# Decay rows of a state-space scan: from matmuls into PSUM to a DRAM round trip and GpSimd

## The reference, cut to what matters

```python
adt = (dt * a).reshape(b, nc, L, g, j)            # decay per token and head
acs = jnp.cumsum(adt, axis=2)                      # running sum in the chunk
tri = jnp.tril(jnp.ones((L, L), dtype=bool))
seg = acs[:, :, :, None] - acs[:, :, None, :]
decay = jnp.exp(jnp.where(tri[None, None, :, :, None, None], seg, -jnp.inf))
cb = jnp.einsum('bclgn,bcsgn->bclsg', cc, bc)
y_diag = jnp.einsum('bclsgj,bcsgjp->bclgjp', cb[..., None] * decay, xdt)
...
y_off = jnp.einsum('bclgn,bcgjpn,bclgj->bclgjp', cc, prev_states, jnp.exp(acs))
```

## Time and profile before

| | |
|---|---|
| median of 3 runs | 1867.87 us (1867.15 to 1870.73) |
| the profiled execution | 1866.71 us, of it span 1864.9 us |
| TensorE's granted clock over the span | 0.995 of full |
| PE busy | 1811.9 us (97%), 11428 matmuls |
| DVE busy | 1301.9 us (70%) |
| ACT busy | 924.2 us (50%) |
| POOL busy | 552.9 us (30%) |
| the stage of the change | 245 to 307 us from the span's start |

### The profile page before, as it was taken

The page is one execution under the profiler, slowest core; times in us unless marked ns, Lnnn a source line. Parts: engine busy times, 40 slices in busy tenths (PEclk is TensorE's granted clock), DMA queues, the critical chain, the costliest instruction groups (busy, mean ns, idle before and its releaser), DMA issues.

```text
span 1864.9 us, 33412 instructions
## 1 busy us (share of the span) xinstructions
PE 1811.9 (97%) x11428; PEld 1576.3 (85%) x11428; DVE 1301.9 (70%) x2376; ACT 924.2 (50%) x1296; POOL 552.9 (30%) x247
## 2 busy tenths in 40 slices
PE   9999999999999989999999999999999999989997
PEld 6899977896878989999999988888886677659996
DVE  4667497775424599357777588888886687867777
ACT  5565544533556534467777543333334474134444
POOL 5867643500668598810000000000000000003333
PEclk9999999999999999999999999999999999999999
DMA  6544433577344467755555787777777880155553
GB/s 213 196 149 143 169 107 102 192 248 240 124 167 152 140 187 220 210 175 179 171 176 175 204 260 233 241 235 235 238 238 256 267 282 19 57 189 183 183 188 113
DMA packets 122841, 347.67 MB, mean 186 GB/s; under 512 B 13904, under 2 KB 46800, under 8 KB 122512
## 3 DMA queue, kind: packets, MB, share of 16 engines
q1 hardware_dynamic: 121248, 339.52, 55.9%
q0 software_dynamic: 1520, 7.21, 1.1%
HBM read 328.84 MB, written 17.83 MB: 186 GB/s over the span
## 4 chain that ended last, share of the span: by engine, by line
PE 82%; DVE 7%; POOL 4%; ACT 3%; issue 3%; DMA 1%; POOLq 0%; ACTq 0%; DVEq 0%
PE banks L915 81%; POOL weight_rest L825 4%; DMA weight_ring<-in_stream 1%; ACT arena L1552 1%; ACT weight_high L1552 1%; PE banks L926 1%; DVE ssd_rest L2150 1%; DVE arena L2320 1%; DVE weight_rest L2124 0%; DVE arena L2691 0%; DVE arena L2806 0%; DVE small L2700 0%; DVE attention_rest L2379 0%; DVE arena L2269 0%; DVE arena L2103 0%
## 5 line engine op out<-in xcount | busy, mean ns | idle before, releaser
L1552 ACT ACTIVATE weight_high<-weight_ring 128x1024 fp32r<-128x1024 f32 x448 | 473.2, 1057 | 451.8 <-PE banks L915 374.4
L825 POOL TENSOR_TENSOR weight_rest<-weight_ring,weight_high 128x1024 fp32r<-128x1024 f32 x181 | 469.5, 2604 | 199.8 <-ACT weight_high L1552 116.4
L2124 DVE TENSOR_TENSOR weight_rest<-weight_ring,weight_high 128x1024 fp32r<-128x1024 f32 x267 | 326.8, 1224 | 165.9 <-ACT weight_high L1552 161.8
L915 PE MATMUL banks<-a_high,weight_high 128*128 128x256 f32 x1216 | 303.8, 288 | 0.1
L915 PE MATMUL banks<-a_rest,weight_high 128*128 128x256 f32 x1216 | 297.8, 283 | 0.0
L915 PEld LDWEIGHTS banks<-a_rest,weight_high 128*128 128x128 f32 x1216 | 233.0, 192 | 0.3 <-issue 0.2
L915 PEld LDWEIGHTS banks<-a_high,weight_high 128*128 128x128 f32 x1216 | 232.6, 191 | 0.6 <-ACT weight_high L1552 0.3
L915 PE MATMUL banks<-weight_high,gated_high 128*128 128x512 f32 x512 | 201.4, 393 | 0.0
L915 PE MATMUL banks<-weight_high,gated_rest 128*128 128x512 f32 x512 | 200.2, 391 | 0.0
L1552 ACT ACTIVATE arena<-banks 128x512 f32<-128x512 f32 (+4 forms) x241 | 161.0, 689 | 65.4 <-PE banks L915 63.4
L915 PE MATMUL banks<-a_high,weight_rest 128*128 128x256 f32 x1216 | 171.9, 284 | 12.4 <-POOL weight_rest L825 12.4
(11 more groups left out here) (319 smaller groups left out, 3223.6 us busy)
## 6 DMA issues: line engine op xcount, KB each, us to landing
weight_ring<-in_stream SPq DMA_DIRECT2D x512, 512.0 KB, 3.5
arena<-in_stream SPq DMA_DIRECT2D x66, 512.0 KB, 3.3
unit_spill<-small SPq DMA_DIRECT2D x128, 128.0 KB, 3.6
scratch<-unit_spill SPq DMA_DIRECT2D x128, 128.0 KB, 3.2
residual<-in_x SPq DMA_DIRECT2D x2, 512.0 KB, 4.3
arena<-in_mem POOLq DMA_DIRECT2D x2, 512.0 KB, 5.1
arena<-in_ctx POOLq DMA_DIRECT2D x2, 512.0 KB, 5.0
arena<-in_keys POOLq DMA_DIRECT2D x1, 1024.0 KB, 5.2
```

The lines of the kernel that those rows point to most:

```text
L825: nc.gpsimd.tensor_tensor(w_lo[:, e % 2, :], raw(e)[0], w_hi[:, e % 2, :], ALU.subtract).then_inc(S["rest_ready"], 1)
L915: return nc.tensor.matmul(out, lhsT, rhs, start=start, stop=stop, skip_group_check=True)
L1552: return nc.scalar.activation(out, in_, f, **kw)
L2124: tt(w_lo[:, e % 2, :], raw(e)[0], w_hi[:, e % 2, :], ALU.subtract).then_inc(S[ready], 1)
```

## The change

The "row" matmuls, VectorE's `decay_rows` and GpSimd's `adt_rows` go. In their place:

- TensorE does two small matmuls ("acr") behind "acs", ADT of a chunk times `upto`, which give the running sums with a head per partition (32 x 128 for each chunk). ScalarE evacuates them to ACR, between two weight splits and the second half of the attention's exponentials.
- GpSimd stores ACR to DRAM in two DMAs (`decay_rows`, 8 x 1024 floats), behind the rest split of tile 17 of `in_xbc`.
- For each group GpSimd issues a DMA that reads the group's 1024 floats for all 128 partitions into DROW (`scratch`, two buffers, 512 KB each time). Those of groups 0 and 1 are issued behind tile 20.
- GpSimd does the subtraction and the bound by 0 (`decays(k)`, 8 instructions of 128 x 128, SBUF to SBUF), then issues the load of group k + 2. The rest split of `mem_k` 0 comes behind `decays(1)`.
- ScalarE's exponential waits for `decays_made` and no longer for the row banks. The turns of the banks are kept: where a row took one, the turn is left out.

```diff
@@ plan_banks
     B.job("acs")
+    B.job("acr")
...
-            turn("row", *groups[k], 0)
-            turn("row", *groups[k], 1)
+            next(turns)
+            next(turns)
@@ gpsimd
-            def adt_rows(k):
+            def load_decay_rows(k):
+                if k > 1:
+                    pool.wait_ge(S["decays_made"], k - 1)
+                pool.dma_start(DROW[:, k % 2].rearrange("p h l -> p (h l)"),
+                               decay_rows[k].partition_broadcast(P)).then_inc(rows_in[k % 2], 16)
+            def decays(k):
                 c, g = k // SG, k % SG
+                pool.wait_ge(rows_in[k % 2], 16 * (k // 2 + 1))
                 if k > 1:
-                    arrived(pool, ("row", (k - 2) // SG, (k - 2) % SG, 1))
-                nc.gpsimd.tensor_copy(ADTB[:, k % 2], bc(ADT[:, c, 8 * g:8 * g + 8], 2, P)).then_inc(S["adtb_ready"], 1)
+                    arrived(pool, ("yd", (k - 2) // SG, (k - 2) % SG))
+                for j in range(8):
+                    h = 8 * g + j
+                    ins = nc.gpsimd.tensor_scalar(EM[:, k % 2, j, :], DROW[:, k % 2, j, :], ACS[:, c, h:h + 1], 0.0,
+                                                  ALU.subtract, ALU.min)
+                ins.then_inc(S["decays_made"], 1)
...
-            pool.wait_ge(S["adt_ready"], 1)
-            adt_rows(0)
-            for n in range(18, 24):
+            freed(pool, ("acr",))
+            for c in range(TT):
+                pool.dma_start(decay_rows[c * SG:(c + 1) * SG].rearrange("g (h l) -> (g h) l", h=8),
+                               ACR[:, c, :]).then_inc(rows_out, 16)
+            for n in range(18, 21):
                 split_rest(E0["in_xbc"] + n)
-            adt_rows(1)
-            split_rest(E0["mem_k"])
-            for k in range(2, TT * SG):
-                adt_rows(k)
+            pool.wait_ge(rows_out, 16 * TT)
+            load_decay_rows(0)
+            load_decay_rows(1)
+            for n in range(21, 24):
+                split_rest(E0["in_xbc"] + n)
+            pool.wait_ge(S["acs_ready"], 1)
+            for k in range(TT * SG):
+                decays(k)
+                if k + 2 < TT * SG:
+                    load_decay_rows(k + 2)
+                if k == 1:
+                    split_rest(E0["mem_k"])
@@ tensor
+            b = claim(("acr",))
+            for c in range(TT):
+                ins = mm(b[0:32, c * P:(c + 1) * P], ADT[:, c, :], C("upto"))
+            filled(ins, ("acr",))
...
-                if k < len(groups):
-                    c, g = groups[k]
-                    pe.wait_ge(S["adtb_ready"], k + 1)
-                    for half in range(2):
-                        b = claim(("row", c, g, half))
-                        for j in range(4):
-                            ins = mm(b[:, hsl(j)], ADTB[:, k % 2, 4 * half + j, :], C("upto"))
-                        filled(ins, ("row", c, g, half))
@@ scalar
+            evacuate(("acr",), ACR.rearrange("p c l -> p (c l)"), src=lambda b: b[0:32, 0:T])
             attention_exp(1)
...
-                for half in range(2):
-                    freed(act, ("row", k // SG, k % SG, half))
+                act.wait_ge(S["decays_made"], k + 1)
                 func(EM[:, k % 2], EM[:, k % 2], ACT.Exp).then_inc(S["seg_exp"], 1)
@@ vector
             for k in range(n_groups + 1):
-                if k < n_groups:
-                    decay_rows(k)
```

## The result

The changed kernel is slower: 1880.55 us as a median (1878.44 to 1882.88, four runs) against 1868.14 (1867.15 to 1870.73, four runs), and that is clear of noise: a ratio of 1.0061 with a 95% interval of 1.0045 to 1.0077. On another chip it came to 1877.63 against 1868.33, 1.0047 (1.003 to 1.0064). The forecast was 1858 with a range of 1852 to 1868.5. The profiled execution has 1879.72 us, 13.0 more than that of the kernel before. I look for these 13 us first.

What follows compares the result with a forecast made beforehand. It took TensorE to bound the loop's second half, VectorE and ScalarE the first. Terms: -13.8 + 0.8 + 2.0 + 0.9 = -10.1 us, from 1866.71 to 1856.6; median 1.16 higher, rounded 1858, range 1852 to 1868.5.

Steps and rivals of the forecast that it cites:

- The subtraction: One GpSimd `tensor_scalar` of 128 columns in the loop: 0.40 us, so 3.2 us a group.
- The waits for VectorE: GpSimd waits for VectorE's instructions with two SBUF inputs, 0.6 us a group, making `decays` 3.8 us.
- two loops through buffers, EM's and DROW's: Buffer reuse over two groups: EM's 8.1 us against TensorE's 9.12, DROW's 9.8 us.
- the slow-GpSimd rival: GpSimd's subtractions hold up the loop: old beat equalled at 1.0 us each, 1886 at 1.5 us; chance 0.11.
- The middle rival: Loads come late, or a subtraction takes 0.6 to 0.9 us, shrinking the gain: 1862 to 1868; chance 0.18.
- the DROW loop: Load issue, landing and subtractions take 9.8 us in two groups, 0.33 a group over TensorE: 2.0 us over six groups.
- its store and its first loads: DRAM store and loads of groups 0 and 1, ahead of the loop: covered by rest splits, cost nothing.
- TensorE's side: Without the row matmuls a group costs TensorE 4.56 us; the loop ends at 293.3, not 307.1, 13.8 us earlier.
- "Acr" and what goes with it: Added matmuls on TensorE, 0.5 us, and their evacuation on ScalarE, 0.4: 0.9 us slower.
- The port: Up to 260 us VectorE waits for GpSimd's rest split of `mem_k` 0 and one decay: 0.8 us slower.

Runs made afterwards that it cites:

- experiment 8: Changed kernel with GpSimd subtracting four heads of a group and ScalarE four, loads from GpSimd: 1863.95 us, ratio 0.9978; run again 1865.32 us, 0.9976.
- the best version: Changed kernel with four subtractions a group on GpSimd, four on ScalarE, loads of groups 2 to 7 from ScalarE's queue: 1859.71 us, ratio 0.9952.
- experiment 2: Changed kernel with VectorE subtracting from the loaded rows, GpSimd only issuing loads, rest split of `mem_k` 0 moved ahead: 1865.70 us, ratio 0.9994.
- experiment 7: Changed kernel with ScalarE making difference and bound from the loaded rows in SBUF, GpSimd only issuing loads: 1863.95 us, ratio 0.9982.
- experiment 4: Changed kernel with another form of GpSimd instruction in most groups, to price each form: one time, 1857.68 us.
- experiment 1: Changed kernel with two GpSimd instructions of 1024 columns a group in place of eight of 128: 1869.36 us, ratio 1.0013.
- experiment 6: Kernel before, row matmuls kept, with ScalarE making difference and bound from PSUM in place of VectorE: 1868.63 us, ratio 1.0001.
- experiment 11: Changed kernel with the loads of groups 2 to 7 issued from ScalarE's queue, all subtractions on GpSimd: 1872.32 us, ratio 1.0035.
- experiment 10: Changed kernel with 6, 6 and 8 filler matmuls in TensorE's last three waits only: 1873.93 us, ratio 1.0034.
- experiment 9: Filler matmuls before each group's products in the changed kernel: 1882.90 us, ratio 1.0072; in groups 0 to 3 of experiment 8's kernel: 1869.25 us, 1.0005.

## Why the prediction was wrong

- **The subtraction.** The forecast took 0.40 us from bounds of 0.24 and 0.46; it is 0.69 by itself, from start to start, and 0.857 on the average in the loop. This is the term that failed. The bounds came from rows of 256 and 1024 columns of a copy and of a two-input form. A `tensor_scalar` with two operations costs some 3.3 ns a column and 0.2 us fixed, and no row of the trace before holds that price. The sentence "I have no reason that excludes 1 us" was right, and the upper bound should have followed it. The Trainium skill (GPSIMD Engine Reference, Engine selection) calls one-input work on GpSimd "roughly line-rate"; the trace disagrees for this form, 0.70 us for 128 columns where VectorE takes 0.278 us.
- **The waits for VectorE** were priced at 0.6 us a group and are 1.2. The mechanism was the forecast's own, the size was half.
- **The bound that was not written down.** The forecast checked two loops through buffers, EM's and DROW's, and both contain `decays` once in two groups. It never checked that GpSimd does all groups one after another: a group costs it 8c, the waits for VectorE, and 0.95 us for the issue and the wait ahead of it. With the forecast's own figures, 3.8 + 0.57 = 4.4 us, the missing bound did no harm, being under 4.56; with the measured ones it is 5.5 + 1.2 + 0.95 = 7.7 us, over the old beat of 6.44. Even with only the 0.40 put right, the forecast's figures would have given 5.5 + 0.6 + 0.57 = 6.7 us, over it too, but no line of the forecast adds them up. The break-even with that beat is c = (6.44 - 0.95 - 1.2) / 8 = 0.54 us, and not the 1.0 of the slow-GpSimd rival, which thus had the right mechanism and the wrong place for the threshold. Had the forecast's 0.40 been right, the sum with the measured waits would be 5.4 us a group, an estimate, under the old beat but over TensorE's 4.65.
- **The middle rival**, a subtraction of 0.6 to 0.9 us, was priced at 1862 to 1868 by the DROW loop. The size came true and the time did not, for the same missing bound.
- **DROW, the loop expected to be last.** It is not, and its 2.0 us in the sum were not there in this form: the load lands in 4.7 us beside 7 us of subtractions, and no engine waited for it. The DRAM trip is hidden, as forecast for its store and its first loads.
- **TensorE's side was right.** Without the rows a group costs it 4.65 us from start to start (forecast 4.56), seen once GpSimd was relieved (experiment 8), and then the tile starts at 299 to 300 in two profiles and at 303.7 in a third (forecast 296 to 298), and the time is 1859.7 in the best version (forecast 1858). A gain of 8 us was there to be had; the change spent it on GpSimd. That this version comes so near to the forecast is partly luck, since it is another kernel than the one that was forecast. "Acr" and what goes with it, 0.9 us in the sum, made 0.9.
- **The port**, 0.8 us forecast, from the rest split of `mem_k` 0 and one decay beside VectorE. VectorE did lose time, but to rest splits and not to subtractions. The two scalings ahead of the loop, one at a time, in the changed kernel and before:

```profile
240.13 4.09 DVE L2126 TENSOR_SCALAR arena<-arena,stat 128x1024 f32<-128x1024 f32 x1
239.26 1.06 DVE L2103 TENSOR_SCALAR arena<-arena,stat 128x1024 f32<-128x1024 f32 x1
240.24 2.90 DVE L2103 TENSOR_SCALAR arena<-arena,stat 128x1024 f32<-128x1024 f32 x1
```

  In the kernel before the first fell for the most part between two rest splits and took 1.06 us. Behind the two first loads three splits now run back to back from 236.50 to 243.65, and the scaling ends 0.57 us behind the last. With the second, 0.86 us now, the pair takes 4.87 for 3.88, and this 1.0 us is in the chain. The rest split of `mem_k` 0 (258.44) stretches one L2312 from 0.69 to 3.20 us. The sign was right and the size near it; the place was another. The Trainium skill (SBUF — State Buffer, Who interferes with whom) names `tensor_scalar` among the forms that can take the ports shared with GpSimd; the trace agrees, by 4.09 us beside the splits against 1.06 between them. In experiments 2 and 7 the split of `mem_k` 0 stands behind these three, both scalings meet one, and the pair takes 6.9 us.
- **The clock** was not in the forecast. In the changed kernel it is 0.50 behind the last subtraction, and the way from there to the tile takes 7.9 us where it takes 4.9 at 1.00: 3.0 us, and 1.2 behind it.
- **Sum of the loss**, against the profiled execution of before: 0.9 us ahead of the stage, 4.5 in the stage, net of what TensorE gained (7.5 less the 3.0), mainly GpSimd's beat, 4.2 from the clock at the end of the loop, 3.3 from a later dip that doesn't need the change; 12.9 of 13.0. By medians the loss is 9.3 on one chip and 12.4 on the other.

What stays open: why the clock falls in one execution at 500 us and not in the next, and why it is at 0.50 in the stage of the half-and-half kernel for 17 us in one profile and for 10 in the other, which goes with 4.6 us of the stage.

## What to carry to other kernels

Work that moves to an idle engine needs its own line in the sum: instructions times duration plus waits and DMA issues, against the beat of the loop, besides the loops through buffers. Where the trace has no row of the same operation, form and size on that engine, the size is not known to better than a factor of two, and the threshold at which the answer flips should be computed first and compared with that factor. Instructions that meet the other engine on shared ports need their waits in the same line: the average of a group hid that 53 of 64 took 0.70 to 0.79 us and 11 took 0.94 to 2.08. How much is moved is a choice too: with half of the work on GpSimd and half on ScalarE the kernel was 3 to 4 us faster than before, and 8 with the loads from ScalarE's queue; with all of it on GpSimd it was 9 to 12 us slower.

## What the runs showed of the hardware

- GpSimd, 128 partitions, 128 columns, medians of experiment 4: 0.29 us for a copy, and for `tensor_scalar` 0.52 with one operation on a constant, 0.61 with one on a pointer, 0.65 with two on constants, 0.71 with two and a pointer; with two on constants 1.10 for 256 columns and 3.64 for 1024. The two-input subtraction of 1024 columns with one input broadcast takes 1.9 us, half of the scalar form with two operations (experiment 1).
- In the changed kernel 11 of 64 GpSimd subtractions took 0.94 to 2.08 us and not 0.70, each beside a VectorE instruction with two SBUF inputs or, once, a scaling.
- The same subtraction takes 0.28 us on VectorE from SBUF (experiment 2) and 0.38 to 0.39 on ScalarE (as Relu with bias) from PSUM or SBUF (experiments 6 and 7).
- A GpSimd DMA that depends on GpSimd's own last instruction adds 0.30 us of wait to its 0.6 us of issue, in all six turns of the changed kernel. From ScalarE's queue the issue took 0.33 us in the chain (experiment 11).
- TensorE's granted clock stood at 0.50 from 306 to 318 us after waits of 1.3 to 2.3 us a turn, and at 1.00 with twenty small matmuls in the last three waits (experiment 10). Fillers did not always do that: at 250 to 260 us it was 0.66 with them and 0.75 without (experiments 9 and 8). Single dips to 0.66 and 0.83 over 10 us occur in kernels with and without the change; one at 0.66 cost 3.4 us of the same code (experiment 6 against the kernel before).
